# The end of the second layer: the wait of the first output products, and two row tiles scaled there for the third layer

## The chip, the cores and the metric

The kernel runs on one core of a Trainium2 chip. The metric is the device time of one execution in microseconds (us); smaller is better. A core has a matrix engine (TensorE, PE in the profile), a vector engine (VectorE, DVE), a scalar engine (ScalarE, ACT), a general engine (GpSimd, POOL) and SyncE (SP), which here issues the transfers. Each runs its own instructions in the order in which the program gives them; they meet at semaphores. Working memory (SBUF) has 128 partitions; matrix products land in eight banks (PSUM) of 128 x 512 floats.

## What is computed

Three layers over a sequence of 1024 rows of 1024 floats: retention, attention with a sliding window of 128, and a layer with two attention branches (forgetting attention and differential attention). Cut to what matters here:

```python
def swa_layer(x, ...):                 # second layer; its last lines
    o = o.reshape(b, s, SWA_Q_WIDTH) * jax.nn.silu(gate)
    return x + o @ w_out

def rms_norm(x, g, eps):
    xf = x.astype(jnp.float32)
    y = xf * lax.rsqrt(jnp.mean(xf * xf, axis=-1, keepdims=True) + eps)
    return (y * g.astype(jnp.float32)).astype(x.dtype)

def second_block(x, g_pre, w_in, ...): # third layer; its first lines
    h = rms_norm(x, g_pre[l], NORM_EPS)
    proj = jnp.einsum('bsd,dn->bsn', h, w_in[l])
    qa, ka, va, fa, za, qb, kb, vb, zb, gates = jnp.split(proj, SPLIT_POINTS, axis=-1)
```

## The kernel before

Every row tile has 128 rows, so there are 8 (TILES). A matrix product in full precision is made from parts: each operand is split into a high and a low half, and three products (high x high, low x high, high x low) are added in one bank, over 8 slices of the inner dimension (KT): 24 instructions of 128 x 512 (products, L91). ACT makes the high halves, DVE the low ones.

**The second layer's end** (window_layer). The attention runs over 32 items (ITEMS: 4 groups of heads x 8 row tiles), n counts the steps, and PE's order is written out by hand: in step n stand scores(n - 2), then project(n) in three pieces (slices 0 to 2, 3 to 5, 6 to 7), and between the pieces transpose_probs(n - 3), values(n - 3), the transposes of the queries of item n - 1 and of the gate of item n - 3. project(n) writes bank p_proj[n % 2]; DVE reads it in norm_queries(n) (qn_done, L1567) and put_gate(n) (gate_done, L1562). From step 32 on output(m) takes the place of project: the product of the attention's result with w_out, for 16 pairs of a row tile and a half of the columns (the list outputs: tiles 0 to 3 in their first half, then in their second, then tiles 4 and 5, then 6 and 7), again into p_proj[m % 2]. output(m) waits for the low half of its rows (o_lo, out_low, L1618) and, from m = 2 on, for add_rows(m - 2) on DVE (x_added, L1627), which adds the bank to the rows of x. output(0) and output(1) wait for qn_done and gate_done of all 32 items.

There are four places for row tiles of x (x_rows). When a tile is whole, ACT squares it, POOL makes its 1/root of the mean (rstd_next, for the third layer), and SP stores it in x2 and loads tile t + 4 into its place. SP's queue there is in this order: the last of eight loads of the attention's result (oT_raw, each behind an o_lo), the load of the third layer's first weights (w_turns, 2 MB), then for each tile the store, a wait for its end, and the load of tile t + 4.

**The third layer's start** (branches_layer, attend). The two layers are separate blocks of the program, with a barrier of all engines between them, and SP comes to it when all of x2 is stored. The start loads x2 again, all 8 tiles, with the row of g_pre copied to all partitions (g_rows, 512 KB) behind the first. DVE scales each tile by rstd and g_rows (scale_rows, L2393), PE transposes it (norm, 8 transposes of 128 x 128, L2081), ACT and DVE split the result into halves (norm_high, norm_low, L2387). Beside it the weights are split (split_high L2248, split_low L2380). PE's order is norm(t), forget(t - 2) (the narrow products for the forget gate, L2095 and L2096), project(t - 2). DVE's order is scale_rows(0), four split_low, scale_rows(1), and then for each t norm_low(t) and scale_rows(t + 2), with the other split_low behind t = 0 and 1.

## Time and profile before

| | us |
|---|---|
| median of 3 runs | 2387.35 (2385.57 to 2387.75) |
| the profiled execution | 2388.51 |
| its span in the trace | 2386.7 |
| PE busy | 2277.0 |
| DVE busy | 1116.3 |
| ACT busy | 881.3 |

The span goes from the first to the last instruction of the profiled execution. All times of the rows below are us from its start. The second layer lasts in the trace from 901.4 to 1351.0; the third follows. Instructions of one line that follow on each other are merged into one row, with their number. PEclk is the clock granted to PE, as a share of full speed.

### The profile page before, as it was taken

The page shows a single profiled execution, that of the slowest core. Times are in us where ns is not written, and L with a number is a line of the kernel's source. Part 1 is how long each engine was busy: PE and PEld are TensorE (multiplying, and loading weights), DVE is VectorE, ACT ScalarE, POOL GpSimd, SP SyncE. Part 2 cuts the span into 40 slices and gives each one's busy share as a digit, 9 for nine tenths or more (in the row PEclk, how much of TensorE's full clock was granted, in tenths as well). Part 3 has the DMA queues.
Part 4 walks back from the last instruction along what each step waited for, and adds up shares of the span by engine and source line. Part 5 has one row for each costly group of instructions (what it writes and reads, how often), then busy time and mean ns, then how long its engine had stood idle before and what let it go on. Part 6 is the DMA issues. An engine that isn't in the chain of part 4 may idle for free. (4 is left out here: it accounts for less than half of the span.)

```text
span 2386.7 us, 32879 instructions
## 1 busy us (share of the span) xinstructions
PE 2277.0 (95%) x11898; PEld 1826.6 (77%) x11898; DVE 1116.3 (47%) x3122; ACT 881.3 (37%) x2274; POOL 213.5 (9%) x313
## 2 busy tenths in 40 slices
PE   6999999999999998999989799999999999999998
PEld 5888888888887887677767686777777777788876
DVE  5254264354362124454544326576665766633342
ACT  4043151341342113445543224454544545522232
POOL 1000000000000001121110000010010100101013
PEclk9999999999999999999999899999999999999999
DMA  4111111111145113011133501110111102424322
GB/s 144 38 49 58 55 57 51 53 48 60 44 168 195 71 62 115 10 52 49 52 109 113 177 26 59 60 44 8 60 44 60 43 9 78 136 71 124 97 98 88
DMA packets 125293, 175.07 MB, mean 73 GB/s; under 512 B 7577, under 2 KB 73177, under 8 KB 123617
## 3 DMA queue, kind: packets, MB, share of 16 engines
q1 hardware_dynamic: 119088, 157.39, 20.3%
q10 hardware_dynamic: 6064, 15.84, 1.8%
q8 instruction: 84, 1.38, 0.2%
q14 instruction: 57, 0.46, 0.1%
HBM read 143.79 MB, written 29.42 MB: 73 GB/s over the span
## 5 line engine op out<-in xcount | busy, mean ns | idle before, releaser
L91 PE MATMUL heads_p_ps<-ret_w_second_hi_sb,ret_hT_hi_sb 128*128 128x512 f32 x384 | 150.2, 391 | 2.0 <-DVE ret_w_second_lo_sb L613 2.0
L91 PE MATMUL heads_p_ps<-ret_w_second_lo_sb,ret_hT_hi_sb 128*128 128x512 f32 x384 | 149.4, 389 | 0.0
L91 PE MATMUL heads_p_ps<-ret_w_second_hi_sb,ret_hT_lo_sb 128*128 128x512 f32 x384 | 149.4, 389 | 0.0
L91 PE MATMUL att_proj_ps<-br_w_second_hi_sb,br_hT_hi_sb 128*128 128x512 f32 x320 | 136.9, 428 | 2.8 <-DVE br_w_second_lo_sb L2380 2.8
L91 PE MATMUL att_proj_ps<-br_w_second_hi_sb,br_hT_lo_sb 128*128 128x512 f32 x320 | 126.2, 394 | 0.0
L91 PE MATMUL att_proj_ps<-br_w_second_lo_sb,br_hT_hi_sb 128*128 128x512 f32 x320 | 126.1, 394 | 0.0
L2329 ACT ACTIVATE br_x_sb<-br_x_sb,att_max_neg_sb 128x256 f32<-128x256 f32 (+7 forms) x128 | 97.8, 767 | 27.7 <-DVE att_max_neg_sb L2553 27.7
L91 PEld LDWEIGHTS heads_p_ps<-ret_w_second_hi_sb,ret_hT_hi_sb 128*128 128x128 f32 x384 | 72.0, 187 | 18.5 <-issue 3.9
L91 PEld LDWEIGHTS heads_p_ps<-ret_w_second_lo_sb,ret_hT_hi_sb 128*128 128x128 f32 x384 | 72.2, 188 | 15.1
L91 PEld LDWEIGHTS heads_p_ps<-ret_w_second_hi_sb,ret_hT_lo_sb 128*128 128x128 f32 x384 | 72.1, 188 | 14.8
L91 PE MATMUL swa_p_ps<-swa_w_first_hi_sb,swa_hT_hi_sb 128*128 128x512 f32 x160 | 70.8, 442 | 10.5 <-DVE swa_qn_sb L1567 7.0
L2148 PEld LDWEIGHTS att_t_ps<-all_ident_sb,br_x_sb 128*128 128x128 f32 x432 | 47.4, 141 | 38.5 <-DVE br_x_sb L2570 18.6
L401 POOL TENSOR_TENSOR heads_o_rstd_sb<-heads_o_ms_sb,heads_minus_half_sb 128x1 f32<-128x1 f32 x32 | 17.6, 550 | 644.9 <-ACT heads_o_ms_sb L600 644.9
L507 ACT ACTIVATE ret_w_second_hi_sb<-early_w_kv_sb 128x512 fp32r<-128x512 f32 x52 | 28.5, 622 | 126.1 <-PE heads_p_ps L91 126.1
L2148 PE MATMUL att_t_ps<-all_ident_sb,br_x_sb 128*128 128x128 f32 x432 | 66.7, 282 | 6.6 <-DVE br_x_sb L2570 5.5
L91 PEld LDWEIGHTS att_proj_ps<-br_w_second_hi_sb,br_hT_hi_sb 128*128 128x128 f32 x320 | 61.1, 191 | 14.2 <-issue 3.5
L91 PEld LDWEIGHTS att_proj_ps<-br_w_second_lo_sb,br_hT_hi_sb 128*128 128x128 f32 x320 | 60.5, 189 | 13.7
L91 PE MATMUL att_proj_ps<-br_w_diff_hi_sb,br_hT_hi_sb 128*128 128x512 f32 x160 | 66.9, 418 | 4.2 <-ACT att_vz_fox_sb L2226 3.8
L566 ACT ACTIVATE heads_v_sb<-heads_p_ps 128x512 f32<-128x512 f32 x32 | 19.1, 598 | 140.2 <-PE heads_p_ps L91 140.0
L2039 POOL TENSOR_TENSOR att_o_pow_sb<-att_o_ms_sb,att_minus_half_sb 128x2 f32<-128x2 f32 x32 | 31.5, 985 | 415.5 <-ACT att_o_ms_sb L2311 415.5
L91 PE MATMUL att_proj_ps<-br_w_fox_hi_sb,br_hT_hi_sb 128*128 128x512 f32 x160 | 68.3, 427 | 0.4 <-ACT br_qkT_fox_sb L2235 0.2
L91 PEld LDWEIGHTS att_proj_ps<-br_w_second_hi_sb,br_hT_lo_sb 128*128 128x128 f32 x320 | 61.2, 191 | 8.2
(543 smaller groups left out, 6362.6 us busy)
## 6 DMA issues: line engine op xcount, KB each, us to landing
early_w_kv_sb<-a_w_blocks SPq DMA_DIRECT2D x28, 1024.0 KB, 5.2
all_w_block_sb<-w_turns SPq DMA_DIRECT2D x12, 2048.0 KB, 8.7
br_y_raw_sb<-branch_yT_dram SPq DMA_DIRECT2D x32, 512.0 KB, 4.2
ret_o_dram<-early_x_rows_sb ACTq DMA_DIRECT2D x32, 256.0 KB, 2.4
all_w_block_sb<-swa_turns SPq DMA_DIRECT2D x4, 2048.0 KB, 8.8
heads_o_rows_sb<-ret_o_dram ACTq DMA_DIRECT2D x6, 1024.0 KB, 5.5
x_dram<-early_x_rows_sb SPq DMA_DIRECT2D x12, 512.0 KB, 2.8
heads_v_sb<-x SPq DMA_DIRECT2D x8, 512.0 KB, 4.4
```

Source lines behind the costliest of these rows:

```text
L91: mm = pe.matmul(out, rows[a], w[b], start=(k == 0 and a + b == 0), stop=(k == KT - 1 and b == 1))
L401: pool.tensor_tensor(o_rstd[:, t % 2:t % 2 + 1], o_ms[:, t % 2:t % 2 + 1], minus_half[:], ALU.pow).then_inc(orstd_done, 1)
L507: act.activation(w_at(kind)(k)[0], w_raw[:, k % HALF, :], ACT.Copy).then_inc(w_hi, 1)
L566: act.activation(v[:, t, :], p_proj[t % 2][:], ACT.Copy).then_inc(v_copied, 1)
L2039: pool.tensor_tensor(o_pow[:], o_ms[:], minus_half[:], ALU.pow).then_inc(opow_done, 1)
L2148: tr = pe.transpose(p_tr[b][:, j * P:(j + 1) * P], probs[:, t % 2, a, (lo + j) * P:(lo + j + 1) * P], ident[:])
L2329: act.activation(part, part, ACT.Exp, bias=max_neg[:, t % 2, a:a + 1], scale=SCALE, accum_out=p_sum[:, t % 2, a:a + 1]).then_inc(exp_done, 1)
```

## The change

The waits of the first two output products for qn_done and gate_done ask for ITEMS - 1 + m items in place of all: output(0) for 31, the last one that used its bank, output(1) for 32.

Tiles 0 and 1 of x are scaled for the third layer in the second: scale_ahead(t), on DVE behind add_rows(6) and add_rows(7), reads x_rows and writes x_scaled, which lies where the third layer has x[:, 0:2] (until then the copies of the probabilities lie there, so it waits for the last values). g_rows is loaded in the second layer, ahead of w_turns on SP's queue, into the place of weights that are used up, and stays there for the third layer. The reload of the places of tiles 0 and 1 waits for their scaling too (ahead_done). In the third layer the loads of tiles 0 and 1 and of g_rows are gone; PE's norm(0) and norm(1) wait for nothing; and on DVE scale_rows(t + 2) now stands ahead of norm_low(t).

```diff
+    early["g_rows"] = mem.over("v_high", "g_rows", P, DIM, further=4 * 2 * DIM)
...
             for t in range(ITEMS - LOADS, TILES):
                 load_out(t)
+            sp.wait_ge(kv_done, TILES)
+            sp.dma_start(g_rows[:], dram["g_pre_2"].broadcast_to([P, DIM])).then_inc(g_in, 16)
             sp.wait_ge(wo_lo, 2 * KT)
             sp.dma_start(w_raw[:], kt_view(dram["w_turns_2"][0])).then_inc(next_in, 16)
...
                         sp.wait_ge(sq_done, t + 1)
+                        if t < 2:
+                            sp.wait_ge(ahead_done, t + 1)
                         load_rows(t + X_ROWS, t % X_ROWS)
...
                     if m < 2:
-                        pe.wait_ge(qn_done, ITEMS)
-                        pe.wait_ge(gate_done, ITEMS)
+                        pe.wait_ge(qn_done, ITEMS - 1 + m)
+                        pe.wait_ge(gate_done, ITEMS - 1 + m)
...
+            def scale_ahead(t):
+
+                dve.wait_ge(rstd_done, t + 1)
+                dve.wait_ge(g_in, 16)
+                dve.wait_ge(pv_done, ITEMS)
+                dve.scalar_tensor_tensor(x_scaled[:, t], x_rows[t], rstd_next[:, t:t + 1], g_rows[:], ALU.mult, ALU.mult).then_inc(ahead_done, 1)
+
             for m in range(AHEAD - 1, len(outputs)):
                 add_rows(m)
                 if AHEAD <= m < TILES:
                     out_low(m)
+                if m in AT:
+                    scale_ahead(AT.index(m))
...
-            for t in range(TILES):
+            for t in range(2, TILES):
                 sp.dma_start(x[:, t, :], dram["x2"][t * P:(t + 1) * P, :]).then_inc(x_in[t], 16)
-                if t == 0:
-                    sp.dma_start(g_rows, dram["g_pre_2"].broadcast_to([P, DIM])).then_inc(g_in, 16)
+                if t == 2:
                     sp.dma_start(w_f_raw[:], kt_view(dram["w_forget_2"])).then_inc(wf_in, 16)
...
             def norm(t):
 
-                pe.wait_ge(xs_done, t + 1)
+                at_least(pe, xs_done, t - 1)
                 at_least(pe, hT_done, t - 1)
...
             first = Turn(True, None, 0)
-            dve.wait_ge(g_in, 16)
-            scale_rows(0)
             split_low(first, range(0, 4))
-            scale_rows(1)
             for t in range(TILES):
-                norm_low(t)
                 if t + 2 < TILES:
                     scale_rows(t + 2)
+                norm_low(t)
...
+            early["x_scaled"] = mem.over("w_kv", "x_scaled", P, 2, DIM)
```

(AT is (6, 7).) In the rows of the order below, heads_x_more_sb holds the places of row tiles 0 and 1, early_x_rows_sb those of tiles 2 and 3, and swa_hT_lo_sb the low half of the attention's result.

DVE at the end of the second layer, from add_rows(6) to the end of the block, before:

```order
L1627 TENSOR_TENSOR early_x_rows_sb<-swa_p_ps,early_x_rows_sb 128x512
L1618 TENSOR_TENSOR swa_hT_lo_sb<-swa_bias_sb,swa_hT_hi_sb 128x8x128
L1627 TENSOR_TENSOR early_x_rows_sb<-swa_p_ps,early_x_rows_sb 128x512
L1618 TENSOR_TENSOR swa_hT_lo_sb<-swa_bias_sb,swa_hT_hi_sb 128x8x128
L1627 TENSOR_TENSOR heads_x_more_sb<-swa_p_ps,heads_x_more_sb 128x512 x4
L1627 TENSOR_TENSOR early_x_rows_sb<-swa_p_ps,early_x_rows_sb 128x512 x4
```

and after:

```order
L1635 TENSOR_TENSOR early_x_rows_sb<-swa_p_ps,early_x_rows_sb 128x512
L1626 TENSOR_TENSOR swa_hT_lo_sb<-swa_bias_sb,swa_hT_hi_sb 128x8x128
L1692 SCALAR_TENSOR_TENSOR early_x_scaled_sb<-heads_x_more_sb,all_rstd_sb,heads_g_rows_sb 128x1024
L1635 TENSOR_TENSOR early_x_rows_sb<-swa_p_ps,early_x_rows_sb 128x512
L1626 TENSOR_TENSOR swa_hT_lo_sb<-swa_bias_sb,swa_hT_hi_sb 128x8x128
L1692 SCALAR_TENSOR_TENSOR early_x_scaled_sb<-heads_x_more_sb,all_rstd_sb,heads_g_rows_sb 128x1024
L1635 TENSOR_TENSOR heads_x_more_sb<-swa_p_ps,heads_x_more_sb 128x512 x4
L1635 TENSOR_TENSOR early_x_rows_sb<-swa_p_ps,early_x_rows_sb 128x512 x4
```

Two scalings have come in behind the second and the fourth row, each ahead of the next addition.

SP at the end of the second layer, from the last loads of the attention's result, before:

```order
L1149 DMA swa_bias_sb<-swa_oT_dram 128x8x128 x3
L1173 DMA all_w_block_sb<-w_turns_2 128x8x512
L1178 DMA x2_dram<-heads_x_more_sb_58 128x1024
L1120 DMA heads_x_more_sb_58<-x1_dram 128x1024
L1178 DMA x2_dram<-heads_x_more_sb_58 128x1024
```

and after:

```order
L1153 DMA swa_bias_sb<-swa_oT_dram 128x8x128 x3
L1177 DMA heads_g_rows_sb_61<-g_pre_2 128x1024
L1179 DMA all_w_block_sb<-w_turns_2 128x8x512
L1184 DMA x2_dram<-heads_x_more_sb_59 128x1024
L1124 DMA heads_x_more_sb_59<-x1_dram 128x1024
L1184 DMA x2_dram<-heads_x_more_sb_59 128x1024
```

The load of g_rows stands ahead of the weights, the store of tile 0 and the reload of its place.

DVE at the start of the third layer, up to the last low halves of the first weights, before:

```order
L2393 SCALAR_TENSOR_TENSOR br_x_sb<-br_x_sb,all_rstd_sb,att_qkT_diff_sb 128x1024
L2380 TENSOR_TENSOR br_w_fox_lo_sb<-all_w_block_sb,br_w_fox_hi_sb 128x512 x4
L2393 SCALAR_TENSOR_TENSOR br_x_sb<-br_x_sb,all_rstd_sb,att_qkT_diff_sb 128x1024
L2387 TENSOR_TENSOR br_hT_lo_sb<-att_s_ps,br_hT_hi_sb 128x4x128 x2
L2393 SCALAR_TENSOR_TENSOR br_x_sb<-br_x_sb,all_rstd_sb,att_qkT_diff_sb 128x1024
L2406 TENSOR_TENSOR att_w_f_sb<-att_w_f_raw_sb,att_w_f_sb 128x8x8
L2380 TENSOR_TENSOR br_w_second_lo_sb<-all_w_block_sb,br_w_second_hi_sb 128x512 x2
L2387 TENSOR_TENSOR br_hT_lo_sb<-att_s_ps,br_hT_hi_sb 128x4x128 x2
L2393 SCALAR_TENSOR_TENSOR br_x_sb<-br_x_sb,all_rstd_sb,att_qkT_diff_sb 128x1024
L2380 TENSOR_TENSOR br_w_second_lo_sb<-all_w_block_sb,br_w_second_hi_sb 128x512 x2
```

and after:

```order
L2395 TENSOR_TENSOR br_w_fox_lo_sb<-all_w_block_sb,br_w_fox_hi_sb 128x512 x4
L2408 SCALAR_TENSOR_TENSOR br_x_sb<-br_x_sb,all_rstd_sb,heads_g_rows_sb 128x1024
L2402 TENSOR_TENSOR br_hT_lo_sb<-att_s_ps,br_hT_hi_sb 128x4x128 x2
L2418 TENSOR_TENSOR att_w_f_sb<-att_w_f_raw_sb,att_w_f_sb 128x8x8
L2395 TENSOR_TENSOR br_w_second_lo_sb<-all_w_block_sb,br_w_second_hi_sb 128x512 x2
L2408 SCALAR_TENSOR_TENSOR br_x_sb<-br_x_sb,all_rstd_sb,heads_g_rows_sb 128x1024
L2402 TENSOR_TENSOR br_hT_lo_sb<-att_s_ps,br_hT_hi_sb 128x4x128 x2
L2395 TENSOR_TENSOR br_w_second_lo_sb<-all_w_block_sb,br_w_second_hi_sb 128x512 x2
```

Two of four scalings are gone from this piece, and the other two stand ahead of the low halves of their step. PE's instructions are the same and in the same order everywhere; only its waits differ.

## Rows read from the trace of the kernel before

**Rows 1.** The page: busy time of TensorE and its share of the span.

```profile
PE 2277.0 (95%) x11898; PEld 1826.6 (77%) x11898; DVE 1116.3 (47%) x3122; ACT 881.3 (37%) x2274; POOL 213.5 (9%) x313
```

**Rows 2.** Waits of PE: waited for, us in total, times, longest.

```profile
PE att_s_ps L2081 <- DVE br_x_sb L2393: 13.5, 3, 11.5
PE swa_p_ps L91 <- DVE swa_qn_sb L1567: 7.0, 1, 7.0
```

**Rows 3.** Timeline of PE, 1245 to 1272: start, us, line, operation [idle before, releaser].

```profile
1245.14 0.80 PE L91 MATMUL swa_p_ps<-swa_w_first_hi_sb,swa_hT_hi_sb 128*128 128x512 f32 x1 [7.03 <-DVE swa_qn_sb L1567]
...
1251.75 1.08 PE L1307 MATMUL swa_o_ps<-early_w_kv_sb,swa_v_all_sb 128*64 128x256 f32 x8
...
1266.00 0.47 PE L91 MATMUL swa_p_ps<-swa_w_first_hi_sb,swa_hT_hi_sb 128*128 128x512 f32 x1 [1.38 <-DVE swa_hT_lo_sb L1618]
...
1271.18 1.08 PE L1307 MATMUL swa_o_ps<-early_w_kv_sb,swa_v_all_sb 128*64 128x256 f32 x8
```

**Rows 4.** Timeline of DVE, 1237 to 1250.

```profile
1237.99 1.23 DVE L1618 TENSOR_TENSOR swa_hT_lo_sb<-swa_bias_sb,swa_hT_hi_sb 128x1024 fp32r<-128x1024 f32 x1 [0.25 <-ACT swa_hT_hi_sb L1459]
...
1244.66 0.42 DVE L1567 TENSOR_TENSOR swa_qn_sb<-swa_p_ps,swa_q_rstd_sb 128x256 f32<-128x256 f32 x1
1249.79 0.69 DVE L1595 COPY early_w_kv_sb<-swa_t_ps 128x512 f32<-128x512 f32 x1 [4.71 <-PE swa_t_ps L1292]
```

**Rows 5.** Timeline of DVE, 1298 to 1320.

```profile
1298.64 1.23 DVE L1618 TENSOR_TENSOR swa_hT_lo_sb<-swa_bias_sb,swa_hT_hi_sb 128x1024 fp32r<-128x1024 f32 x1 [0.48 <-ACT swa_hT_hi_sb L1459]
...
1310.51 0.69 DVE L1627 TENSOR_TENSOR heads_x_more_sb<-swa_p_ps,heads_x_more_sb 128x512 f32<-128x512 f32 x1 [5.20 <-DMA heads_x_more_sb<-x_dram]
...
1319.23 0.69 DVE L1627 TENSOR_TENSOR heads_x_more_sb<-swa_p_ps,heads_x_more_sb 128x512 f32<-128x512 f32 x1 [2.49 <-PE swa_p_ps L91]
```

**Rows 6.** Timeline of SP's transfers at both places: start of issue, us of issue.

```profile
1295.54 1.57 SPq L1178 DMA_DIRECT2D x_dram<-heads_x_more_sb  x1
1306.54 0.33 SPq L1120 DMA_DIRECT2D heads_x_more_sb<-x_dram  x1
...
1351.01 0.32 SPq L1967 DMA_DIRECT2D br_x_sb<-x_dram  x1
1351.38 0.42 SPq L1969 DMA_DIRECT2D att_qkT_diff_sb<-g_pre  x1
```

**Rows 7.** Timeline of PE at the start of the third layer.

```profile
1357.86 1.97 PE L2081 MATMUL att_s_ps<-all_ident_sb,br_x_sb 128*128 128x128 f32 x8 [11.46 <-DVE br_x_sb L2393]
...
1363.85 1.97 PE L2081 MATMUL att_s_ps<-all_ident_sb,br_x_sb 128*128 128x128 f32 x8 [0.42 <-DVE br_x_sb L2393]
...
1368.89 0.77 PE L91 MATMUL att_proj_ps<-br_w_fox_hi_sb,br_hT_hi_sb 128*128 128x512 f32 x1
```

**Rows 8.** Timeline of DVE at the start of the third layer.

```profile
1356.51 1.28 DVE L2393 SCALAR_TENSOR_TENSOR br_x_sb<-br_x_sb,all_rstd_sb,att_qkT_diff_sb 128x1024 f32<-128x1024 f32 x1 [9.39 <-DMA att_qkT_diff_sb<-g_pre]
...
1361.32 1.28 DVE L2387 TENSOR_TENSOR br_hT_lo_sb<-att_s_ps,br_hT_hi_sb 128x512 fp32r<-128x512 f32 x2
...
1367.44 1.29 DVE L2380 TENSOR_TENSOR br_w_second_lo_sb<-all_w_block_sb,br_w_second_hi_sb 128x512 fp32r<-128x512 f32 x2
```

**Rows 9.** Timeline of ACT at the start of the third layer.

```profile
1351.02 2.19 ACT L2248 ACTIVATE br_w_fox_hi_sb<-all_w_block_sb 128x512 fp32r<-128x512 f32 x4 [2.72 <-PEq L137]
```

**Rows 10.** The eight loads of row tiles in the third layer.

```profile
DMA to landing us min/median/max: 3.3/8.4/10.7
```

**Rows 11.** Timeline of PE at the start of the second layer.

```profile
901.42 1.94 PE L1233 MATMUL swa_s_ps<-all_ident_sb,heads_x_more_sb 128*128 128x128 f32 x8 [4.80 <-PEq L137]
```

**Rows 12.** Windows of PE: from:to, us, busy (instructions), granted clock, DMA share, GB/s.

```profile
1245.00:1249.00 4.00, 3.86 (x12) 0.60 1.07 378
...
1357.80:1369.00 11.20, 9.08 (x41) 0.50 0.84 318
```

**Rows 13.** Chain of waits, third layer: the products of the first two row tiles.

```profile
1369.03 8.20 PE att_proj_ps L91 x24
...
1379.78 5.61 PE att_t_ps L91 x24
```

More of the change, by code:

```diff
@@ L1088, in window_layer @@
         (sq_done, ms_done, rstd_done) = mem.sems("sq_done", "ms_done", "rstd_done")
+        g_in, ahead_done = mem.sems("g_in", "ahead_done")
+        x_scaled, g_rows = early["x_scaled"], early["g_rows"]
         def turn_w(turn, k):
@@ L1111, in window_layer @@
         AHEAD = 4
+        AT = (6, 7)
         LOADS = ITEMS - TILES + 2
@@ L1682, in _, with branches_layer @@
                     out_low(m)
-def branches_layer(nc, ident, dram, w_raw, stats, y_post):
+                if m in AT:
+                    scale_ahead(AT.index(m))
+def branches_layer(nc, ident, dram, w_raw, stats, g_rows, y_post):
     yT_dram = nc.dram_tensor("branch_yT_dram", [2 * PAIRS, P, SEQ], F32, kind="Internal").ap()
@@ L1714, in w_at @@
             return [part[:, k % (KT // 2), :] for part in (w_first[fox] if k < KT // 2 else w_second)]
-        attend(nc, x, ident, dram, hT, w_raw, w_at, stats[1], qkT_fox, gates_0, yT_dram, y_raw, w_br_raw, ahead_in, w_first, y_post)
+        attend(nc, x, ident, dram, hT, w_raw, w_at, stats[1], qkT_fox, gates_0, yT_dram, y_raw, w_br_raw, ahead_in, w_first, g_rows, y_post)
 class Turn:
@@ L1764, in in_turns, with attend @@
         body(turn, prev, following)
-def attend(nc, x, ident, dram, hT, w_raw, w_at, rstd, qkT_fox, gates_0, yT_dram, y_raw, w_br_raw, ahead_in, m_mem, y_post):
+def attend(nc, x, ident, dram, hT, w_raw, w_at, rstd, qkT_fox, gates_0, yT_dram, y_raw, w_br_raw, ahead_in, m_mem, g_rows, y_post):
     c_dram = nc.dram_tensor("fox_c_dram", [FOX_HEADS, SEQ], F32, kind="Internal").ap()
@@ L1840, in attend @@
         lams, lam_prod = lam_mem[:, 0:4 * HD].rearrange("p (n d) -> p n d", n=4), lam_mem[:, 4 * HD:5 * HD]
-        g_rows = qkT[False][:, 0, :]
-        ones = vz[False][0:FOX_HEADS, 4:6, :].rearrange("p t n -> p (t n)")
+        ones = vz[False][0:FOX_HEADS, 0:2, :].rearrange("p t n -> p (t n)")
         f_z, f_a, f_u, f_ln, f_d, f_eq = (c_row[:, 1, n * FW:(n + 1) * FW] for n in range(6))
@@ L1851, in attend @@
         yT_cols, zT_cols = slice(2 * P, 3 * P), slice(3 * P, 4 * P)
-        (const_in, wf_in, g_in, w_in_sem, c_out, c_in, *y_out) = mem.sems(
-            "const_in", "wf_in", "g_in", "w_in", "c_out", "c_in", "y_out0", "y_out1")
+        (const_in, wf_in, w_in_sem, c_out, c_in, *y_out) = mem.sems(
+            "const_in", "wf_in", "w_in", "c_out", "c_in", "y_out0", "y_out1")
         x_in = mem.sems(*(f"x_in{t}" for t in range(TILES)))
@@ L2392, in scale_rows @@
                 dve.wait_ge(x_in[t], 16)
-                dve.scalar_tensor_tensor(x[:, t, :], x[:, t, :], rstd[:, t:t + 1], g_rows, ALU.mult, ALU.mult).then_inc(xs_done, 1)
+                dve.scalar_tensor_tensor(x[:, t, :], x[:, t, :], rstd[:, t:t + 1], g_rows[:], ALU.mult, ALU.mult).then_inc(xs_done, 1)
             first = Turn(True, None, 0)
-            dve.wait_ge(g_in, 16)
-            scale_rows(0)
             split_low(first, range(0, 4))
-            scale_rows(1)
             for t in range(TILES):
-                norm_low(t)
                 if t + 2 < TILES:
                     scale_rows(t + 2)
+                norm_low(t)
                 if t == 0:
@@ L3055, in build @@
                      "x_rows": mem.sb("x_rows", P, 2, DIM), "ssq": mem.sb("ssq", P, TILES), "rstd": mem.sb("rstd", P, TILES)}
+            early["x_scaled"] = mem.over("w_kv", "x_scaled", P, 2, DIM)
             retention_layer(nc, ident, dram, early)
             window_layer(nc, ident, dram, early, stats)
-        branches_layer(nc, ident, dram, w_block, stats, dram["out"])
+        branches_layer(nc, ident, dram, w_block, stats, early["g_rows"], dram["out"])
 def head_blocks(w_in, w_out):
```

## The prediction

> **What bounds the kernel now.** I read the page first. TensorE (PE) is busy for 95% of the span of 2386.7 us [rows 1], so only what makes PE stand still, or run at its lower clock, can be won. The second view is the list of PE's waits, longest first. Two of its entries lie in the stretch that the change touches: 13.5 us for the scaled rows at the start of the third layer and 7.0 us for the normalised queries at the end of the second [rows 2]. The third view is the timeline around both places, engine by engine, to see which instruction of which engine ended last. The rest of PE's time is products that follow on each other, and what is shifted ahead of them shifts them whole, to the end of the program.
>
> **Part 1, the wait of the first output product.** output(0) writes bank p_proj[0], which item 30 was the last to read, but it waits for item 31. PE starts output(0) at 1245.14 after 7.03 us of idle time, so it has stood since 1238.1, released by L1567 [rows 3]; that is norm_queries(31), which ended at 1244.66 + 0.42 = 1245.08 [rows 4]. With the value ITEMS - 1 the item asked for is 30, long done. What is late next is out_low(0) on DVE, 1237.99 + 1.23 = 1239.22 [rows 4], so output(0) can start at 1239.3.
> It doesn't keep this lead of 5.9 us by itself. Between its pieces PE has transpose_probs(29) and values(29), and values(29) needs DVE's copy of the transposed probabilities (L1595), which stands in DVE's queue behind norm_queries(31). DVE's own chain up to that does not depend on output(0) and stays where it is. So: PE's side, measured on the same sequence one product later at full clock, is 1271.18 - 1266.00 = 5.18 us from the start of the output to values [rows 3], which gives 1239.3 + 5.2 = 1244.5. DVE's side is 1245.08 + 0.69 for the copy [rows 4] = 1245.8. The later one counts: values(29) at 1245.8 in place of 1251.75 [rows 3], a gain of **5.95 us**, with PE idle for 1.3 us ahead of it. The same number comes out if PE should run these nine products at its low clock, since DVE's side is the later by 1.3 us. Everything behind, the ACT copies of item 31, out_high, out_low and the output products, hangs on PE from there and moves with it; the loads that these use wait for the same instructions or are on their way by then.
>
> **Part 2, what is added inside the second layer.** On DVE two scalings of 128 x 1024 at 1.28 us each, the time of the same form in the third layer [rows 8]. They stand behind add_rows(6) and add_rows(7), where DVE is idle for 5.2 us ahead of its next addition [rows 5]: cost nothing. Queued behind a scaling that waits for g_in would be add_rows(7), for which output(9) waits; the load of g_rows goes out near 1295, just ahead of w_turns and of the store at 1295.54 [rows 6], and the first scaling comes behind out_low(6), 1298.64 + 1.23 = 1299.9 [rows 5]. At the other place the same load took 5.1 us with a row tile ahead of it (issued 1351.38 [rows 6], used 1356.5 [rows 8]), so here it costs some tenths at most, with a cover of 5 us.
> On SP's queue there is one more load, 512 KB, ahead of the 2 MB of w_turns, the store of tile 0 and the reload of its place with tile 4. These run one behind the other: the store issued at 1295.54 was waited for until 1306.54 [rows 6], and add_rows(8) waited for the reload until 1310.51 [rows 5]. add_rows(8) ends at 1311.2, and output(10) asks for it; its start is its end, 1319.2 [rows 5], less 5.6 us for 24 products at full clock [rows 13], so 1313.6. **Slack 2.4 us.** The load puts 512 KB into a queue that moves 2.5 MB in the 11 us of that wait, so 2.2 us by that rate; and at the other place it landed 2.2 us behind the tile ahead of it (1351.01 + 3.3 = 1354.3 [rows 6, 10], then 1356.5). From above, all of its 5.1 us; from below 0, if the queue has room beside the others. I take 2.2 us, where two rows meet: it fits under 2.4, barely, and PE doesn't wait. With 5.1 it would wait 2.7 us once (output(11) has the same delay, not a second one). ahead_done, for which SP now also waits, is set 4 us or more before the store is done.
>
> **Part 3, the start of the third layer.** Before, PE stands for 11.46 us until 1357.86 [rows 7]: from 1346.4 on 4.6 us until the layers' barrier (SP's first load at 1351.01 [rows 6]), which stays, since it waits for the last store of x2; then tile 0 and g_rows are loaded, tile 0 is scaled by 1357.8. The first projection starts at 1368.89 [rows 7], when DVE has made the last low half of the weights, 1367.44 + 1.29 = 1368.7 [rows 8].
> After: PE's first 16 transposes need nothing. At the start of the second layer the same kind of instruction started with the barrier and took 1.94 us for eight at the low clock [rows 11], so they are done by 1354.7. ACT makes the first four high halves until 1351.02 + 2.19 = 1353.2 [rows 9], and DVE the low ones until 1353.9. Now scale_rows(2) stands ahead of norm_low(0), and with it tile 2's load, now the first in the queue. The shortest landing of a row tile here is 3.3 us [rows 10], which I take for the first: 1354.3. From there DVE runs without a gap, as before: its chain from norm_low(0) at 1361.32 to the last low half at 1368.73 is 7.4 us [rows 8], with two scalings, two norm_low and four low halves in it, and the new order holds exactly the same instructions between the landing and that half. So 1354.35 + 7.4 = 1361.8 on DVE. On PE, norm(2) can go when norm_low(0) is done (two 1.2 us steps behind the landing, 1356.8), and norm(2) with forget(0) takes 1368.89 - 1363.85 = 5.0 us at the low clock [rows 7], so 1361.8 as well. With some 0.3 us for the handovers the projection starts at 1362.2: a gain of **6.7 us**. Bounds: if the first tile lands as late as g_rows did (5.1 in place of 3.3 us), 4.9; if neither handover costs, 7.0. w_forget is issued earlier than before and 1.5 MB less is in the queue, so later tiles don't come later.
>
> **The clock.** PE's granted clock is 0.50, its lower level of 1.2 GHz, through the whole stretch 1357.8 to 1369 though PE is busy 9.08 of 11.2 us in it [rows 12]; the 24 products that follow take 8.20 us and the next 24, at 2.4 GHz, 5.61 [rows 13]. This 2.6 us is the most that a clock already up could add to the gain. After the change PE still stands 4.6 us, has 16 transposes and stands again for 2 us, so I expect the first products at the low level again and count 0. The Trainium skill ("TensorE: Matmul & The Clock Gate", section "Part 4: PE-mode transpose") says that transposes don't count as work for the gate; by it the 16 early transposes bring no warm start, and the sum stays as it is, where a gate that did count them would give 2.6 us more. Rows 12 agree: transposes and the narrow products of forget did not raise it.
>
> **The sum.** 5.95 + 0 + 6.7 = 12.65 us. The profiled execution took 2388.51 us (span 2386.7), 1.16 above the median of the three runs, 2387.35. So 2375.9 for such an execution, and 2374.7 us for the median.
>
> **Rivals.**
> (1) The clock is up early in the first projection, because the products start at another moment or the low stretch is shorter: up to 2.6 us more, 2372.1. For it: at the other place (1245.14) the mean clock of the first 4 us of products is 0.60 [rows 12], so the rise came after 3.2 us of them; in the third layer the 2.6 us lost on 24 products stand for 5.2 us. Against: the pauses ahead of it stay.
> (2) The queue: g_rows costs 5.1 rather than 2.2 us and output(10) waits 2.7 us, or the first tile lands 1.8 us later than taken, or both: gain 8.2 to 10.9, so 2376.5 to 2379.2. For it: the slack is only 2.4 us. Against: the waits are single and not repeated.
> (3) One part doesn't do what it says: values(29) waits for something else than DVE's copy, or the barrier comes no earlier; 5.95 or 6.7 alone, 2380.7 to 2381.4.
> (4) No change: both shifts are taken back by a later fixed transfer. Nothing in PE's waits shows one behind 1346; 2387.
> (5) Slower: the same place as (2), output(10) behind the reload of tile 4 on SP's queue. Each microsecond of g_rows beyond 2.4 costs one; from 2.4 + 12.65 = 15.05 us the kernel is slower than before, and at 20 us, four times the 5.1 seen at the other place, it is at 2392.3. Such a load would also be longer than the wait of 11 us for all that is now in that queue [rows 6].
>
> **How the numbers follow.** Forecast 0.62, (1) 0.12, (2) 0.16, (3) 0.05, (4) 0.02, (5) 0.03. The clock also falls and rises at other places of the third layer, which all move by 12.65 us; each may gain or lose a microsecond or two, and the three runs differ by 2.2 us. The range from 2371.0 to 2378.8 takes in the forecast, (1), and most of (2). A measurement of this kernel can tell 0.2%, 4.8 us, from no change; (1), (2), (3) and the forecast are all faster by more. Faster 0.95, within 0.2% 0.02, slower 0.03.
>
> **What would show it.** Right: output(0) starts about 1239.3, behind out_low(0); PE idle about 1.3 us ahead of values(29), released by the DVE copy; products of the second layer ending near 1340.5; no PE wait at output(10); add_rows(8) later by about 2 us against the products; PE's first transposes at the barrier near 1345.1; the first projection near 1356.2, 11 us behind the barrier rather than 18. Wrong: a PE wait for add_rows in the output loop, a first row tile that lands over 4 us after its issue, or a projection that waits for the ACT halves behind w_forget.

## The result, and the profile after

The changed kernel takes 2372.76 us (median of 4 runs, 2370.31 to 2374.49), the kernel before 2386.74 us on the same chip (4 runs, 2385.57 to 2387.75): a ratio of 0.9943, 95% interval 0.9931 to 0.9954, or 14.0 us less. The forecast of 2374.7 us was 1.9 us too high, and the time lies inside the range. The profiled execution of after took 2370.31 us. Its page begins with the span and the busy time of each engine, to be held against [rows 1]: PE does the same work, is busy for 4.5 us less in all, and for half a per cent more of a shorter span (95.4% before, 95.9% after).

```profile
span 2368.5 us, 32878 instructions
...
PE 2272.5 (96%) x11898; PEld 1824.8 (77%) x11898; DVE 1116.9 (47%) x3122; ACT 880.8 (37%) x2274; POOL 213.2 (9%) x313
```

The list of PE's waits after the change (waited for, us in total, times, longest) answers [rows 2]. The 13.5 us for the scaled rows and the 7.0 us for the normalised queries are gone. In their place stand small waits: one for the copy ahead of values (the profile names no releaser), one for a low half of the output product, and 2.3 us for the first norm_low of the third layer. The first two lines below are sums over four waits each; before they were 4.5 and 3.5 us over three, so one wait in each is new. The pause of 4.7 us between the layers stays.

```profile
PE swa_o_ps L1315 <- issue: 5.5, 4, 1.5
PE swa_p_ps L91 <- DVE swa_hT_lo_sb L1626: 4.9, 4, 1.4
...
PE att_s_ps L2096 <- PEq L137: 4.7, 1, 4.7
...
PE att_s_ps L2096 <- DVE br_hT_lo_sb L2402: 2.3, 1, 2.3
```

**Where the time went.** I cut each trace at the same five instructions of the kernel: the start of scores(30), the start of values(29), SP's first load of the third layer (which marks the barrier), and the starts of the first and the second projection of the third layer. All stage times below are worked out from such starts, us:

| trace | to scores(30) | scores(30) to values(29) | to the barrier | barrier to first projection | to second projection | to the end | span |
|---|---|---|---|---|---|---|---|
| before | 1236.97 | 14.78 | 99.26 | 17.88 | 10.75 | 1007.11 | 2386.7 |
| after | 1232.68 | 8.81 | 99.28 | 11.02 | 10.16 | 1006.58 | 2368.5 |
| e1_wait_only | 1233.34 | 8.81 | 99.26 | 17.81 | 10.12 | 1008.10 | 2377.4 |
| e2_ahead_only | 1233.07 | 16.21 | 99.29 | 11.03 | 9.89 | 1007.21 | 2376.7 |
| e3_rows_early | 1231.71 | 8.82 | 99.34 | 15.76 | 9.50 | 1005.21 | 2370.3 |
| e4_more_loads | 1233.51 | 8.82 | 105.87 | 11.07 | 10.19 | 1006.94 | 2376.4 |
| e5_project_first | 1233.75 | 8.82 | 99.25 | 4.43 | 12.70 | 1006.49 | 2365.4 |
| e6_old_dve_order | 1234.44 | 8.82 | 99.25 | 10.66 | 10.37 | 1007.30 | 2370.8 |
| e7_before_again | 1233.96 | 16.24 | 99.27 | 17.82 | 9.94 | 1009.90 | 2387.1 |
| e8_wait_again | 1234.33 | 8.81 | 99.27 | 17.95 | 10.31 | 1008.08 | 2378.8 |
| e9_after_again | 1235.16 | 8.81 | 99.27 | 11.03 | 10.31 | 1009.73 | 2374.3 |

Two columns hold the change: the second (14.78 to 8.81, 5.97 us less) and the fourth (17.88 to 11.02, 6.86 us less). The fourth repeats within 0.14 us among kernels with the same code in it, and the second within 0.01 us with the new wait. With the old wait the second doesn't repeat: 14.78 in before, 16.2 in e2 and e7. The spans of before and after differ by 18.2 us, 4.2 more than the medians do. That is the first column (4.3), in which no code was changed: e7 is the kernel before again, and there it is 1233.96.

**Part 1 in the trace of after.** PE's timeline (start, duration, engine, line, output and inputs, in brackets the idle time before it), to be held against [rows 3]:

```profile
1232.68 1.14 PE L1290 MATMUL swa_s_ps<-swa_k_all_sb,swa_qT_sb 64*128 64x256 f32 x8
...
1235.18 0.47 PE L91 MATMUL swa_p_ps<-swa_w_first_hi_sb,swa_hT_hi_sb 128*128 128x512 f32 x1 [1.36 <-DVE swa_hT_lo_sb L1626]
...
1241.49 0.87 PE L1315 MATMUL swa_o_ps<-early_w_kv_sb,swa_v_all_sb 128*64 128x256 f32 x6 [1.08 <-issue]
```

and DVE's, to be held against [rows 4]:

```profile
1240.37 0.42 DVE L1575 TENSOR_TENSOR swa_qn_sb<-swa_p_ps,swa_q_rstd_sb 128x256 f32<-128x256 f32 x1
1240.71 0.68 DVE L1603 COPY early_w_kv_sb<-swa_t_ps 128x512 f32<-128x512 f32 x1
```

output(0) starts 2.5 us behind scores(30), released by out_low, no longer by the normalised queries. values(29) starts at 1241.49, a tenth behind the end of DVE's copy, 1240.71 + 0.68 = 1241.39. So this copy sets it, though the profile writes "issue" for the 1.08 us that PE stands. The copy still stands right behind norm_queries(31) in DVE's queue.

**Part 2.** SP's timeline of after, for [rows 6], with the new load of g_rows first, then the store of tile 0, the reload of its place, and the first load of the third layer:

```profile
1284.65 0.57 SPq L1177 DMA_DIRECT2D heads_g_rows_sb<-g_pre  x1
...
1285.74 0.94 SPq L1184 DMA_DIRECT2D x_dram<-heads_x_more_sb  x1
...
1297.47 0.34 SPq L1124 DMA_DIRECT2D heads_x_more_sb<-x_dram  x1
...
1340.77 0.32 SPq L1983 DMA_DIRECT2D br_x_sb<-x_dram  x1
```

DVE's timeline of the same place, for [rows 5]: the first scaling, and add_rows(8) behind the reload.

```profile
1289.98 1.29 DVE L1692 SCALAR_TENSOR_TENSOR early_x_scaled_sb<-heads_x_more_sb,all_rstd_sb,heads_g_rows_sb 128x1024 f32<-128x1024 f32 x1 [0.37 <-DMA heads_g_rows_sb<-g_pre]
...
1301.57 0.69 DVE L1635 TENSOR_TENSOR heads_x_more_sb<-swa_p_ps,heads_x_more_sb 128x512 f32<-128x512 f32 x1 [5.33 <-DMA heads_x_more_sb<-x_dram]
```

g_rows is there 5.3 us after its issue, and the scaling waits 0.37 us for it. From values(29) to add_rows(8) it was 1310.51 - 1251.75 = 58.76 us before [rows 3, 5] and is 1301.57 - 1241.49 = 60.08 us now: the reload comes 1.3 us later against the products. PE doesn't wait; the third column is 99.28 against 99.26.

**Part 3.** PE's timeline at the start of the third layer, for [rows 7]:

```profile
1340.80 3.65 PE L2096 MATMUL att_s_ps<-all_ident_sb,br_x_sb 128*128 128x128 f32 x16 [4.67 <-PEq L137]
1346.78 1.94 PE L2096 MATMUL att_s_ps<-all_ident_sb,br_x_sb 128*128 128x128 f32 x8 [2.33 <-DVE br_hT_lo_sb L2402]
...
1351.79 0.77 PE L91 MATMUL att_proj_ps<-br_w_fox_hi_sb,br_hT_hi_sb 128*128 128x512 f32 x1
...
1359.37 1.04 PE L2096 MATMUL att_s_ps<-all_ident_sb,br_x_sb 128*128 128x128 f32 x8
```

DVE's, for [rows 8]: tile 2 is scaled, and the last low half of the weights.

```profile
1344.15 1.28 DVE L2408 SCALAR_TENSOR_TENSOR br_x_sb<-br_x_sb,all_rstd_sb,heads_g_rows_sb 128x1024 f32<-128x1024 f32 x1 [0.21 <-DMA br_x_sb<-x_dram]
...
1350.28 1.28 DVE L2395 TENSOR_TENSOR br_w_second_lo_sb<-all_w_block_sb,br_w_second_hi_sb 128x512 fp32r<-128x512 f32 x2
```

The 16 transposes of the two tiles that are ready start with the barrier. Tile 2 is scaled 3.4 us after its load was issued (1340.77 to 1344.15). The last low half ends at 1350.28 + 1.28 = 1351.56, and norm(2) with forget(0) lets PE go at 1351.79: the two chains end within 0.23 us of each other.

The windows of PE in after (from:to, length, busy time and instructions, granted clock as a share of 2.4 GHz, share of the DMA engines, GB/s), for [rows 12]. The clock stays up over the shorter pause of part 1. In the third layer it is at 1.2 GHz for the whole 10.9 us ahead of the first projection, though PE is busy in 8.56 of them, and rises only within the projection.

```profile
1233.00:1241.40 8.40, 6.05 (x34) 1.00 0.28 65
...
1340.80:1351.70 10.90, 8.56 (x40) 0.50 0.90 287
1351.80:1359.40 7.60, 7.60 (x26) 0.72 0.73 235
```

### The profile page after: what moved, and what is told of

It reads as the page before. It is cut to its first block and busy times, and to the rows that moved or that the text cites. A ratio compares the mean times of both kernels' runs of the same rounds, so it can differ in the third digit from the quotient of the medians.

```text
span 2368.5 us, 32878 instructions
## 1 busy us (share of the span) xinstructions
PE 2272.5 (96%) x11898; PEld 1824.8 (77%) x11898; DVE 1116.9 (47%) x3122; ACT 880.8 (37%) x2274; POOL 213.2 (9%) x313
## 5 line engine op out<-in xcount | busy, mean ns | idle before, releaser
L91 PEld LDWEIGHTS att_proj_ps<-br_w_second_lo_sb,br_hT_hi_sb 128*128 128x128 f32 x320 | 60.1, 188 | 13.5
```

Of the source, the lines that this page charges most:

```text
L91: mm = pe.matmul(out, rows[a], w[b], start=(k == 0 and a + b == 0), stop=(k == KT - 1 and b == 1))
```

## The experiments

The theory is the prediction's sum: two independent shifts, 5.95 us from the wait of the first output product and 6.7 us from the tiles scaled ahead, with the added load inside its slack. The rivals are that one part alone brings it all, that the load in SP's queue eats the gain, and that a clock which is up earlier makes it.

**e1: the wait alone.** On the kernel before:

```diff
-                        pe.wait_ge(qn_done, ITEMS)
-                        pe.wait_ge(gate_done, ITEMS)
+                        pe.wait_ge(qn_done, ITEMS - 1 + m)
+                        pe.wait_ge(gate_done, ITEMS - 1 + m)
```

> The kernel before with only the changed waits of the first two output products. Theory (the wait for item 31 was the last thing late, and the DVE copy of the probabilities is next): values(29) comes 5.95 us earlier, about 4.4 us after the first piece of the output product could start, released behind the DVE copy; the third layer's start is as before (17.9 us from the barrier to the first projection); total 6.0 us less than before, about 2380.8. Rival (the gain is lost at the output loop, where the reload of tile 4 becomes late): total under 3 us less, with a wait of PE in the loop. Rival (the stage gains from the clock as well and the parts overlap): over 8 us less.

Measured 2382.66 us (11 runs, 2379.23 to 2384.19) beside 2386.4 for before: ratio 0.9985 (0.9976 to 0.9994), 3.7 us less. PE's timeline of e1:

```profile
1233.34 1.13 PE L1282 MATMUL swa_s_ps<-swa_k_all_sb,swa_qT_sb 64*128 64x256 f32 x8
...
1242.15 1.08 PE L1307 MATMUL swa_o_ps<-early_w_kv_sb,swa_v_all_sb 128*64 128x256 f32 x8 [1.08 <-issue]
```

The stage is 8.81 us, as in after to the hundredth, and the third and the fourth column are those of before. So the shift of 5.97 us belongs to this edit alone. The median shows less of it than the 6.0 us expected, between 1.4 and 5.7 us by the interval. e8 returns to that.

**e2: the tiles ahead alone.** The changed kernel with the old waits, that is, the edit of e1 backwards.

> The changed kernel with the old waits of the first two output products (all 32 items). Theory: the first output product waits 7 us for item 31 as before, and the third layer's start keeps its gain: barrier to first projection 11.0 us rather than 17.9, and 0.6 us more in the first projection if the clock rises as early as in the changed kernel; total 6.9 to 7.5 us less than before, about 2379.5. Rival (both parts share a gain, by the clock's moments): more than 9 us or less than 5 us less than before. The two parts alone should add up to the 14.0 us measured, within 1.5.

Measured 2379.35 us (2377.88 to 2381.63): ratio 0.9969 (0.9958 to 0.9980), 7.1 us less. The fourth column is 11.03 us. The timeline of e2 shows the old wait back, and the window behind it the clock at its lower level:

```profile
1241.24 0.79 PE L91 MATMUL swa_p_ps<-swa_w_first_hi_sb,swa_hT_hi_sb 128*128 128x512 f32 x1 [7.04 <-DVE swa_qn_sb L1575]
```

```profile
1241.00:1245.00 4.00, 3.76 (x9) 0.50 1.05 372
```

In before the products behind this wait ran at 0.60 [rows 12]. Here the rise comes later and the stage is 16.21 us, not 14.78. Neither part needs the other: each shift shows whole in the trace of the kernel that has only this part. The medians of the two parts add up to 3.7 + 7.1 = 10.8 us, which misses the 14.0 us by more than the 1.5 that were expected at most; their stages add up to 12.8 us.

**e3: g_rows early, no tile scaled ahead.** The computation is unchanged. The changed kernel without the two scalings in the second layer. The third layer loads all eight tiles and scales them in the old order, with g_rows there beforehand:

```diff
-                if m in AT:
-                    scale_ahead(AT.index(m))
...
-            for t in range(2, TILES):
+            for t in range(TILES):
                 sp.dma_start(x[:, t, :], dram["x2"][t * P:(t + 1) * P, :]).then_inc(x_in[t], 16)
...
-                at_least(pe, xs_done, t - 1)
+                pe.wait_ge(xs_done, t + 1)
```

> The changed kernel with g_rows loaded in the second layer, but no tile scaled there: the third layer loads and scales all eight tiles in the order of the kernel before. It tells the early load of the row from the scaling ahead. Theory: the first scaling starts when tile 0 has landed, 3.3 us behind the barrier and not 5.5, and all behind it on DVE moves by 2.2 us: barrier to first projection 15.7 us; total 8.2 us less than before (5.95 + 2.2), about 2378.6. Rival (the load of g_rows was most of what was late): 11 to 12 us from barrier to projection, and the total of the changed kernel. Rival (the tile's own load is late, not the row's): 17.9 us as before.

Measured 2374.25 us (2372.13 to 2379.91): ratio 0.9955 (0.9941 to 0.9969), 12.2 us less. SP's first load and DVE's first scaling in e3:

```profile
1339.87 0.32 SPq L1980 DMA_DIRECT2D br_x_sb<-x_dram  x1
```

```profile
1343.27 1.28 DVE L2405 SCALAR_TENSOR_TENSOR br_x_sb<-br_x_sb,all_rstd_sb,heads_g_rows_sb 128x1024 f32<-128x1024 f32 x1 [7.30 <-DMA br_x_sb<-x_dram]
```

The first tile lands 3.4 us after its issue and is scaled at once, where before DVE went on waiting for g_rows, 5.1 us. The fourth column is 15.76 us: the row of factors alone is 2.1 of the 6.9 us, and the two tiles that need neither load nor scaling are the other 4.7. The total is 4 us better than expected, though. Of that the trace shows 1.25 us in the fifth column and 1.9 in the sixth, where e3's code is that of before. This is the scatter that the last three runs are about.

**e4: three more loads in the queue.** The changed kernel, with 1.5 MB more loaded behind g_rows into places that nobody reads; the computation is unchanged:

```diff
             sp.dma_start(g_rows[:], dram["g_pre_2"].broadcast_to([P, DIM])).then_inc(g_in, 16)
+            sp.wait_ge(s_done, ITEMS)
+            sp.dma_start(g_more[:], dram["g_pre_2"].broadcast_to([P, DIM])).then_inc(more_g, 16)
+            for g in range(SWA_KV):
+                sp.dma_start(k_all[:, g], dram["g_pre_2"].broadcast_to([P, SEQ])).then_inc(more_g, 16)
```

> The changed kernel with three more loads of the same 512 KB row right behind the one of g_rows, into places that are free by then, on the same queue, ahead of w_turns. Nothing reads them. Theory (the reload of tile 4 stands behind all of it and output(10) waits for it beyond a slack of 2.4 us): in the changed kernel the one load moved add_rows(8) by 1.3 us, so four move it by 4 x 1.3 = 5.2, or by 8.8 at the 2.2 us of the prediction; PE then waits 2.8 to 6.4 us ahead of output(10), once, and the kernel is as much slower than the changed one. If the wait passes some 4 us the clock falls too and costs up to 1.5 us more. Rival (the packets of the loads share the queue and cost nothing there): add_rows(8) as in the changed kernel, no wait of PE.

Measured 2378.19 us (2377.05 to 2379.99): ratio 0.9960 (0.9945 to 0.9974), 9.5 us less than before, 4.5 less of a gain than the change. In e4 SP sends the reload out, DVE adds to it, and PE waits for the end of that:

```profile
1303.98 0.33 SPq L1127 DMA_DIRECT2D heads_x_more_sb<-x_dram  x1
```

```profile
1308.25 0.69 DVE L1643 TENSOR_TENSOR heads_x_more_sb<-swa_p_ps,heads_x_more_sb 128x512 f32<-128x512 f32 x1 [11.12 <-DMA heads_x_more_sb<-x_dram]
```

```profile
1309.00 0.77 PE L91 MATMUL swa_p_ps<-swa_hT_hi_sb 128*128 128x512 f32 x1 [4.62 <-DVE heads_x_more_sb L1643]
```

```profile
1309.00:1316.00 7.00, 7.00 (x24) 0.76 0.53 156
```

add_rows(8) starts 1308.25 - (1233.51 + 8.82) = 65.92 us after values(29), in after 60.08: 5.84 us for three loads, 1.95 each. With the 1.32 us of the first load that makes 7.16 us of delay, of which PE waits 4.62, so 2.54 us were free. The slack of 2.4 us in the prediction was right. PE waits once, at output(10), and nowhere behind it, which was the form that rivals (2) and (5) gave to it. The third column grows by 6.59 us: 4.62 of wait, and 2.0 that the products behind it lose, since they start at the lower clock (0.76 in the last window), more than the 1.5 us expected. The medians show less than this stage: 4.5 us between the gains of e4 and of after.

**e5: the first projection ahead of norm(2).** If the third layer now waits for tile 2 and the rest of the weights, the projection of tile 0 can go first, which needs neither:

```diff
             for t in range(TILES + LAG):
+                if t == LAG:
+                    pe.wait_ge(hT_done, 1)
+                    project(first, 0, range(0, 4))
+                    project(first, 0, range(4, KT))
                 if t < TILES:
...
-                if t >= LAG:
+                if t > LAG:
                     pe.wait_ge(hT_done, t - LAG + 1)
...
             for t in range(TILES):
+                if t == 0:
+                    norm_low(0)
+                    split_low(first, range(4, KT))
                 if t + 2 < TILES:
                     scale_rows(t + 2)
-                norm_low(t)
...
+                if t:
+                    norm_low(t)
```

and the same on ACT, where the high halves of the second four parts of the weights come ahead of the forget weights.

> The changed kernel with another order at the third layer's start: PE makes the first projection in two pieces ahead of norm(2) and forget(0); ACT and DVE split all of the first weights ahead of the forget gate's and ahead of the scaling of tile 2. Theory (the 11.0 us from the barrier to the projection are DVE's chain and PE's slow forget products, not loads): the first piece starts about 4.4 us behind the barrier, the second at 6.8; norm(2) and forget(0) run at full clock behind it in 2.7 us; the second projection starts 3 to 4.5 us earlier than in the changed kernel; total 3 to 4.5 us less than it, about 2369. Rival (what is pulled ahead is given back because ACT's copy of the first projection stands behind norm_high(3), or tile 2's load becomes late): less than 1 us.

Measured 2367.85 us (2366.41 to 2369.59): ratio 0.9923 (0.9909 to 0.9937), 18.5 us less than before. It is faster than before, and its median is under that of after, which ran in another comparison; their intervals against before touch at the edge (0.9909 to 0.9937 and 0.9931 to 0.9954). PE's timeline and windows of e5:

```profile
1341.85 3.65 PE L2096 MATMUL att_s_ps<-all_ident_sb,br_x_sb 128*128 128x128 f32 x16 [4.67 <-PEq L137]
1346.25 0.80 PE L91 MATMUL att_proj_ps<-br_w_fox_hi_sb,br_hT_hi_sb 128*128 128x512 f32 x1 [0.75 <-DVE br_hT_lo_sb L2406]
...
1353.74 1.04 PE L2096 MATMUL att_s_ps<-all_ident_sb,br_x_sb 128*128 128x128 f32 x8
...
1356.32 1.09 PE L2096 MATMUL att_s_ps<-all_ident_sb,br_x_sb 128*128 128x128 f32 x8
```

```profile
1346.25:1353.70 7.45, 7.45 (x24) 0.72 0.93 342
1353.74:1358.90 5.16, 5.16 (x49) 1.00 0.57 201
```

PE's wait behind the 16 transposes is 0.75 us now, not 2.33, and the clock comes up within the wide products, ahead of norm(2) and forget(0), which then take 1356.32 - 1353.74 = 2.6 us, not 5.0. From the barrier to the second projection it is 4.43 + 12.70 = 17.1 us, in after 21.2, so 4.1 us less; the medians differ by 4.6 between the two comparisons.

**e6: DVE in the old order.** The changed kernel with norm_low(t) ahead of scale_rows(t+2) again.

> The changed kernel with DVE's old order in the third layer: norm_low(t) ahead of scale_rows(t + 2). Theory (DVE's sum of work up to the last low half is what counts, with the landing of tile 2 hidden either way): norm_low(0) starts 3.3 us behind the barrier rather than 4.6, and the last low half comes 0.2 us earlier or at the same time, since DVE stood 0.2 us for the load; norm(2) on PE starts at the same time, 6.0 us behind the barrier; total within 1 us of the changed kernel. Rival (the order is a part of the gain): barrier to projection 12 us or more.

Measured 2375.39 us (2372.62 to 2376.58), ratio 0.9950 (0.9934 to 0.9967), 12.3 us less than before and not to be told from after. DVE's timeline of e6:

```profile
1345.60 1.28 DVE L2402 TENSOR_TENSOR br_hT_lo_sb<-att_s_ps,br_hT_hi_sb 128x512 fp32r<-128x512 f32 x2
1346.80 1.27 DVE L2408 SCALAR_TENSOR_TENSOR br_x_sb<-br_x_sb,all_rstd_sb,heads_g_rows_sb 128x1024 f32<-128x1024 f32 x1
```

With this order DVE makes norm_low(0) while tile 2 is on its way, and the first projection starts 10.66 us behind the barrier, 0.36 earlier than in after. norm(2) starts 5.6 us behind it, where 6.0 was expected. The new order on DVE, which the prediction took as given, has no share in the gain.

**e7, e8, e9: before, e1 and after once more, together.** The totals of e1 and e3 didn't fit their stages, so these three went side by side, unchanged.

> The kernel before, unchanged, against itself: what a difference of medians is worth, and how much of the profiled execution of before (1237.0 us to scores(30), against 1231.7 to 1234.4 in seven other traces with the same code up to there) is chance. Theory (the moments at which the clock falls and rises in the first 60 us and near 740 us differ from one execution to the next): ratio 1.000 within 0.001, scores(30) between 1232 and 1237. Rival (the changed code shifts the start of the program, as by its size): scores(30) again at 1237.0 within 0.3, and every changed kernel has some 3 us for nothing.

> The changed waits alone once more, since their median fell by 3.7 us where their stage fell by 6.0. Theory (the clock's moments in the third layer take some of it in part of the executions): stage 8.8 us from scores(30) to values(29), start to start, as in the other traces with this edit; total 3.5 to 6 us less than before; the part behind the second projection of the third layer 1007 to 1009 us, with its low stretches at other places than in before. Rival (chance alone): total 5.5 to 6.5 less and that part at 1007.1 as before.

> The changed kernel once more beside the two others of this call, so that its waits alone, and all of it, are compared on the same chip. Theory: 13 to 15 us less than before; barrier to first projection 11.0 us, scores(30) to values(29) 8.8; what the waits alone lack against 6.0 is found behind the first projection, not in these stages. Rival (the parts help each other): the difference between the two kernels is over 10 us with the same stages, and the rest of the third layer is shorter by over 1.5 us.

Beside 2386.61 us for before (21 runs in this comparison), e7 took 2387.33 (2383.60 to 2390.06), ratio 1.0001 (0.9992 to 1.0010); e8 2381.89 (2377.17 to 2383.80), 0.9979 (0.9970 to 0.9988), 4.7 us less; e9 2374.59 (2369.24 to 2376.10), 0.9940 (0.9927 to 0.9954), 12.0 us less. PE's transposes in e7, of the same kernel as before:

```profile
1242.13 0.80 PE L91 MATMUL swa_p_ps<-swa_w_first_hi_sb,swa_hT_hi_sb 128*128 128x512 f32 x1 [7.04 <-DVE swa_qn_sb L1567]
...
1246.14 1.91 PE L1292 MATMUL swa_t_ps<-all_ident_sb,swa_probs_sb 128*128 128x128 f32 x8
```

Three things follow. The first column, 1234.0 in e7 against 1237.0 in before's own trace, moves by 3.0 us with no change in the code, and 1234.0 lies amid the 1231.7 to 1235.2 of the changed kernels, so nothing shows that changed code elsewhere shifts it. The old wait costs more than the one trace of before said: in e7, as in e2, the eight transposes behind it run at the lower clock (1.91 us), and the stage is 16.24 us. And with e9 at 12.0 us, under the 13 to 15 expected, and e8 at 4.7, within its 3.5 to 6, the part that e1 lacks is 7.3 us, near the 6.9 of the fourth column and the 7.1 of e2. That the parts help each other beyond their sum, for which e9 was to differ from e8 by over 10 us, falls.

## Why the prediction was right

**Part 1: right.** Said: output(0) 2.3 us behind scores(30), measured 2.5; PE idle 1.3 us ahead of values(29), measured 1.08, and set by DVE's copy; gain 5.95, measured 5.97 against the same profiled execution. What was mis-sized is what stood on the other side: the prediction took 14.78 us for the old stage from one trace, in which the clock rose after 3.2 us of products. In two other traces with the old wait it rose later, and the stage was 16.2. The gain is 6.0 to 7.4 us, depending on the execution.

**Part 2: the cover was right, the price too high.** The slack of 2.4 us was measured at 2.54 in e4. For the load in SP's queue I took 2.2 us, from a rate of 2.5 MB in 11 us and from how long behind a row tile the same load landed in the third layer; it was 1.3, so PE had over a microsecond to spare. The same rate was nearer to each of the further loads (1.95 us). The scaling's own wait, "some tenths", was 0.37.

**Part 3: right, step by step.** Against the barrier: first landing 3.3, measured 3.4; norm(2) 5.8, measured 6.0; last low half on DVE 10.8, measured 10.8; norm(2) with forget(0) 5.0 us, measured 5.0; first projection 11.2, measured 11.02. The gain was 6.86 us, not 6.7. What the prediction didn't see is that the new DVE order costs 0.36 us (e6), which it had taken as a part of the mechanism.

**The clock: the count of 0 held, its reason only in part.** The first projection took 1359.37 - 1351.79 = 7.58 us, not the 8.2 of [rows 13]. But the fifth column, which holds it, is 10.75, 10.12, 9.94 and 10.31 us in the four traces with the old start of the third layer, and 9.89 to 10.37 in the five with the new one (e3 and e5 left aside), so this belongs to the execution and not to the change. The clock was at 0.50 over the 10.9 us ahead of it. By the Trainium skill ("TensorE: Matmul & The Clock Gate", section "Part 4: PE-mode transpose") transposes don't count as work for the gate. The trace of after agrees, with 16 early transposes among the 8.56 busy microseconds at 0.50. The trace of e3 doesn't. PE's third set of transposes there and its windows:

```profile
1350.60 1.62 PE L2093 MATMUL att_s_ps<-all_ident_sb,br_x_sb 128*128 128x128 f32 x8 [0.42 <-DVE br_x_sb L2405]
```

```profile
1344.60:1351.50 6.90, 4.83 (x20) 0.50 1.00 400
1352.00:1353.90 1.90, 1.90 (x19) 1.00 0.67 212
1353.90:1355.60 1.70, 0.01 (x1) 0.86 0.44 111
```

Behind a pause of 9.38 us PE had nothing but transposes from 1344.61 on, with two short pauses among them. The clock rose in the third set of eight (1.62 us in place of 1.97), and the narrow products behind them ran at 2.4 GHz. PE then waited 1.73 us for a low half of the weights, and in this wait the clock fell again. So the measurement decides against the rule as the prediction used it: transposes alone can be followed by a rise. That there was no early rise in after is what its trace shows; why e3 had one and after had none stays open.

**The rivals.** (1) fell as above: at most 0.6 us of it shows, within the scatter of the fifth column. (2) fell: neither the load nor the first tile was late. (3) fell: e1 and e2 hold one shift each. (4) and (5) fell; e4 shows that (5) is a true mechanism, which four such loads were enough to start (4.62 us of wait) and one was not, though even e4 is 9.5 us faster than before.

**The sum.** By the two stages the change is worth 5.97 + 6.86 = 12.8 us against the profiled execution, and up to 14.3 with the old stage at 16.2. The two comparisons of the medians gave 14.0 and 12.0. The forecast's 12.65 lies between them. That it comes within 2 us of the median is in part luck, since the stages that no edit touched move the total by more than that.

**What stays open.** The medians of the wait alone, 3.7 and 4.7 us less (intervals 1.4 to 5.7 and 2.9 to 7.2), are 1.3 to 2.3 us under its own stage, and 2.7 to 3.7 us under it if the old stage takes 16.2 us. e4 lost 2 us less against after than its stage grew, and e3 was 4 us better than its stages. The sixth column, a thousand microseconds in which none of these kernels differs, spans 1005.2 to 1009.9 us, and 1007.1 to 1009.9 for the kernel before alone. In both untouched stretches, the first column and the sixth, the clock is low at other places from one execution to the next. Windows of PE from the first, 700 to 760 us, of before and then of after:

```profile
700.00:760.00 60.00, 54.87 (x255) 0.94 0.65 219
```

```profile
700.00:760.00 60.00, 56.37 (x272) 1.00 0.68 233
```

And from the sixth, 1880 to 1910 us, of two executions of the kernel before, its own trace and e7:

```profile
1880.00:1910.00 30.00, 26.47 (x145) 1.00 0.23 78
```

```profile
1880.00:1910.00 30.00, 27.44 (x144) 0.94 0.24 78
```

That these low stretches make up the scatter of 4 to 5 us was not worked out. With such a scatter, the remainders of 2 to 4 us can be chance; that they are wasn't shown. e9's expectation, that the lack of the wait alone lies behind the first projection, isn't borne out by e8's trace: its last three stages add up to 1036.3 us, those of e7, the kernel before, to 1037.7. Nor was it settled whether the last thousand microseconds answer to the moment at which the third layer starts.

## What to carry to other kernels

A wait for the last item of a loop, where the first product needs only its own buffer's item, costs what stands between the two; its price is found by asking which queue is the next to be late, and against the same trace that was right to 0.02 us here. At the start of a layer, work that hangs on the first load is worth preparing where its data still lie on the chip, and wide products that are ready should go ahead of transposes and narrow ones, since they cover the landing, and in e5 the clock was up for the rest (another 4.1 us). To measure such a part, cut the traces at the same instructions: three of the stages here repeat within 0.14 us among kernels with the same code in them, where the totals scatter by 4 us. A stage behind a long pause need not: the old wait's took 14.8 us in one execution and 16.2 in two others.

## What the runs showed of the hardware

- PE can be 79% busy for 10.9 us (8.56 of 10.90) with transposes and products of 8 and 16 columns and stay at 1.2 GHz. With 24 products of 512 columns ahead of them (e5) the same instructions ran at 2.4 GHz and took 2.6 us in place of 5.0. In e3 the clock rose within the third set of eight transposes, with no wide product since the pause of 9.38 us ahead of them.
- A pause of 7.0 us was followed by a stretch at the lower clock whose length is not fixed: the same code took 14.78 us in one trace and 16.21 and 16.24 in two others. A pause of 4.62 us (e4) brought the clock down too, for some 2.0 us of loss; the pauses of 1.36 and 1.08 us in after, among wide products, didn't. One of 1.73 us in e3, behind transposes and narrow products, did.
- A load of one row to 128 partitions (512 KB), put ahead of others in the same queue, delayed the addition that waits for the reload behind them by 1.3 us. Three more of them delayed it by 1.95 us each.
- The same kernel's first 1234 us took 1234.0 us in one execution and 1237.0 in another, with no change in the code.
